# Second to fourth head group's queries and keys by a seven-product block scheme in one kernel for a hybrid attention and ConvFFN decoder layer

## What is computed

```
h = rms_norm(x, g_attn)                      # 256 x 2048
proj = h @ w_in                              # 2048 x (3*1024 + 8 + 3*1024 + 2*2048)
qa, ka, va, fa, qb, kb, vb, ga, gb = split(proj)
q_a, k_a = qk_norm(qa), qk_norm(ka)          # per head of 128, likewise q_b, k_b
o_a = fox_attention(q_a, k_a, va, log_sigmoid(fa + b_forget))      # 8 heads
o_b = dilated_attention(q_b, k_b, vb, slopes)                      # 8 heads
merged = sigmoid(ga) * (o_a @ w_br_fox) + sigmoid(gb) * (o_b @ w_br_dil)
x = x + merged @ w_out
x = x + conv_ffn(rms_norm(x, g_ffn))         # w_up 2048 x 11264, 3 taps, silu * val, w_down
```

## Time and profile before

| | |
|---|---|
| median of 3 runs | 1358.18 us (1357.86 to 1358.4) |
| time of the profiled execution | 1357.15 us |
| its span, first to last instruction | 1355.3 us |
| PE, PE weight loads, DVE, ACT, POOL busy | 1349.7, 1117.8, 1080.9, 831.5, 128.9 us |
| DMA | 299.45 MB, 221 GB/s mean |

### The profile page before, as it was taken

One profiled execution on the slowest core, in us unless ns is written; L12 is line 12 of the kernel. 1 busy time (PEld: TensorE's weight loads), 2 busy tenths in 40 slices (PEclk: granted clock), 3 DMA queues, 4 the chain that ended last, 5 costly groups with the idle time before them and its releaser, 6 DMA issues.

```text
span 1355.3 us, 16345 instructions
## 1 busy us (share of the span) xinstructions
PE 1349.7 (100%) x6144; PEld 1117.8 (82%) x6144; DVE 1080.9 (80%) x1320; ACT 831.5 (61%) x1038; POOL 128.9 (10%) x149
## 2 busy tenths in 40 slices
PE   9999999999999999999999999999999999999999
PEld 7888888888888888888888888888888888888887
DVE  6646555678878876657788999898999999999985
ACT  6655445466666654446776767666666666666762
POOL 0101010120111000001010101011110102010100
PEclk9999999999999999999999999999999999999999
DMA  9865555578888645567967988887979898888841
GB/s 344 247 203 170 168 174 170 155 219 233 205 229 230 221 168 175 200 228 226 297 149 292 235 293 222 261 245 210 278 197 286 198 291 181 308 187 282 222 179 62
DMA packets 115679, 299.45 MB, mean 221 GB/s; under 512 B 11656, under 2 KB 12944, under 8 KB 115088
## 3 DMA queue, kind: packets, MB, share of 16 engines
q1 hardware_dynamic: 95072, 241.92, 51.7%
q0 software_dynamic: 16448, 52.44, 22.1%
q10 hardware_dynamic: 4080, 4.05, 0.9%
HBM read 296.26 MB, written 2.11 MB: 220 GB/s over the span
## 4 chain that ended last, share of the span: by engine, by line
PE 99%; DMA 0%; ACT 0%; DVE 0%; issue 0%; SPq 0%; ACTq 0%
PE acc L643 17%; PE acc L645 17%; PE acc L644 16%; PE acc L676 7%; PE acc L680 7%; PE acc L678 7%; PE acc L661 3%; PE acc L665 3%; PE acc L663 3%; PE acc L881 2%; PE acc L883 2%; PE acc L885 2%; PE acc L856 2%; PE acc L858 2%; PE acc L860 2%; PE acc L969 1%
## 5 line engine op out<-in xcount | busy, mean ns | idle before, releaser
L1560 DVE TENSOR_TENSOR w_lo<-raw,w_hi 128x1024 fp32r<-128x1024 f32 x258 | 311.7, 1222 | 146.1 <-ACT w_hi L1133 144.8
L1133 ACT ACTIVATE w_hi<-raw 128x1024 fp32r<-128x1024 f32 x258 | 271.0, 1058 | 207.7 <-PE acc L645 173.8
L643 PE MATMUL acc<-w_hi,actA 128*128 128x512 f32 x856 | 339.7, 397 | 0.1
L645 PE MATMUL acc<-w_hi,actA 128*128 128x512 f32 x856 | 333.9, 390 | 0.0
L644 PE MATMUL acc<-w_lo,actA 128*128 128x512 f32 x856 | 333.2, 389 | 0.0
L645 PEld LDWEIGHTS acc<-w_hi,actA 128*128 128x128 f32 x856 | 160.7, 188 | 34.1
L643 PEld LDWEIGHTS acc<-w_hi,actA 128*128 128x128 f32 x856 | 160.8, 188 | 32.8 <-issue 1.0
L644 PEld LDWEIGHTS acc<-w_lo,actA 128*128 128x128 f32 x856 | 160.9, 188 | 32.2
L1133 ACT ACTIVATE w_hi<-raw_y 128x1024 fp32r<-128x1024 f32 x120 | 127.1, 1061 | 76.8 <-DMA raw_y<-w_in 18.2
L1560 DVE TENSOR_TENSOR w_lo<-raw_y,w_hi 128x1024 fp32r<-128x1024 f32 x120 | 145.2, 1220 | 24.3 <-ACT w_hi L1133 22.5
L1133 ACT ACTIVATE w_hi<-raw_x 128x1024 fp32r<-128x1024 f32 x90 | 95.2, 1059 | 55.6 <-PE acc L645 29.7
(11 more groups left out here) (259 smaller groups left out, 2264.9 us busy)
## 6 DMA issues: line engine op xcount, KB each, us to landing
raw<-w_in SPq DMA_DIRECT2D x126, 512.0 KB, 4.2
raw_x<-w_up SPq DMA_DIRECT2D x44, 512.0 KB, 5.7
raw<-w_down SPq DMA_DIRECT2D x42, 512.0 KB, 5.6
raw_y<-w_up POOLq DMA_DIRECT2D x35, 512.0 KB, 7.2
raw<-w_up SPq DMA_DIRECT2D x30, 512.0 KB, 7.0
raw<-w_out SPq DMA_DIRECT2D x28, 512.0 KB, 4.3
odd<-w_up SPq DMA_DIRECT2D x28, 512.0 KB, 4.4
work<-w_down SPq DMA_DIRECT2D x27, 512.0 KB, 5.1
```

What stands on the lines that cost most here:

```text
L643: nc.tensor.matmul(o, lhsT=a_h, rhs=w_hi[:, s, k, :], start=first and k == 0, stop=False)
L645: mm = nc.tensor.matmul(o, lhsT=a_l, rhs=w_hi[:, s, k, :], start=False, stop=last and k == KU - 1)
L1133: nc.scalar.activation(w_hi[:, n % RING, :, :], src.rearrange("p (k n) -> p k n", k=KU), ACT.Copy).then_inc(hi_done, 1)
L1560: nc.vector.tensor_tensor(w_lo[:, n % RING, :, :], src.rearrange("p (k n) -> p k n", k=KU), w_hi[:, n % RING, :, :].bitcast(f32), ALU.subt ...
```

## The change

The queries and keys of head groups 2 to 4 are no longer two plain rounds each. Each group's query and key columns (512 each) form a pair like those of the gates, so there are seven pairs (three of them before the gates' four), and in the first three the 22 units are followed by eight plain units V0 to V7 for the group's values. Only group 1 keeps its three rounds. The heads of group 1 are attended during the first pair, those of group 2 during the second, the dilated ones of group 3 during the third: scores behind units 2, 12, 19 and V2, the transposes of the probabilities behind units 5, 14, 21 and V4. Squares of the queries hang on unit 20 and of the keys on V3, their scaling on V0 and V4, the transposes behind V1, V2 and V5, V7. The block sums of the activations are made in the first group's rounds and two of them get a buffer of their own (`own_parts`). The decay rows move out of `raw_x` into `work`, and SP no longer waits for them. POOL's queue is reordered by hand. The reserve for POOL's DMA descriptors is set to 8192 bytes per partition. Cut to its core:

```diff
-FF0 = 31
...
-GATE_UNIT = 96
+GATE_UNIT = 24
+PAIRS = 7
...
-    for c in range(4):
+    for c in range(PAIRS):
...
+        if c < QK:
+            units += [("V", c, u) for u in range(UPR)]
...
+SCORES_AT = {("G", 0, 0): 0, ("H", "P5", 1): 1, ("H", "P4", 1): 2, ("V", 2): 3}
+TURN_AT = {("G", 0, 1): 0, ("G", 1, 0): 1, ("G", 1, 3): 2, ("V", 4): 3}
+VALUES_AT = {("H", "P6", 1): 0, ("G", 1, 1): 1, ("V", 1): 2, ("V", 6): 3}
+ROWS_AT = {("V", 1): (0, 0), ("V", 2): (0, 1), ("V", 5): (1, 0), ("V", 7): (1, 1)}
...
+ROUND_BANKS = ((2, 3), (0, 1), (2, 3))
...
+        own_parts = sb("own_parts", [P, 2 * HK * 2 * P], f32r)
...
+        decay_all = work[:, 4096:6144].rearrange("p (h s) -> p h s", s=SEQ)
+        decay = work[0:8, 3072:3072 + SEQ]
...
-            for g in range(GROUPS):
-                base = (0 if g < 2 else DIL_COL) + (g % 2) * NB
-                for m in range(3):
-                    if 3 * g + m > 1:
-                        round_of(3 * g + m, w_in_v, base + 1024 * m)
-            sp.wait_ge(prep_ready, prepared(7))
+            round_of(2, w_in_v, 2048)
...
-            pe.wait_ge(qn_done, 2 * GROUPS)
+            pe.wait_ge(qn_done, 2)
             for n, unit in enumerate(GATES, GATE_UNIT):
                 if unit[0] == "H":
                     gate_product(n, unit[1], unit[2], unit[3])
+                elif unit[0] == "G":
+                    gate_plain(n, unit[1], unit[2], unit[3])
                 else:
-                    gate_plain(n, unit[1], unit[2], unit[3])
+                    _, c, u = unit
+                    if u == 0:
+                        pe.wait_ge(g_c11, c + 1)
+                        pe.wait_ge(g_c21, c + 1)
+                    rows_unit(n, actA, (KU * u, KU * u + 1), (bank[gate_banks(c)[0]], bank[3]), u == 0, u == UPR - 1)
+                c, at = unit[1], place(unit)
+                if c >= QK:
+                    continue
+                if at in SCORES_AT:
+                    j = SCORES_AT[at]
+                    if j == 0:
+                        pe.wait_ge(qkt_done, 4 * (c + 1))
+                        pe.wait_ge(act_evac, c + 1)
+                    attend_scores(q_of(c)[:, j, :], lambda a, b: k_of(c)[:, j, a:b])
+                elif at in TURN_AT:
+                    attend_transpose(4 * c + TURN_AT[at])
+                if at in VALUES_AT:
+                    v, j = v_of(c), VALUES_AT[at]
+                    attend_values(4 * c + j, v[:, 0, j * P:(j + 1) * P], v[:, 1, j * P:(j + 1) * P])
+                if at in ROWS_AT:
+                    if ROWS_AT[at] == (0, 0):
+                        pe.wait_ge(g_c22, c + 1)
+                    transpose_heads(2 * (c + 1) + ROWS_AT[at][0], ROWS_AT[at][1])
 
...
+                elif unit == ("V", c, UPR - 1):
+                    act.wait_ge(used, n + 1)
+                    values_out(c + 1, (bank[gate_banks(c)[0]], bank[3]))
...
+            def squares(c, side):
+                act.wait_ge((g_c11, g_c12)[side], c + 1)
+                act.wait_ge((g_c21, g_c22)[side], c + 1)
+                act.wait_ge(qkt_ready, 2 * (2 * (c + 1) + side))
+                for r in range(RT):
+                    t = nc.scalar.activation(tmp[:, r, :], pair_sum(c, side, r), ACT.Square, scale=xrs[:, r:r + 1])
+                t.then_inc(sq_ready, 1)
 
             for n, unit in enumerate(GATES, GATE_UNIT):
                 gate_sum(n, unit)
                 high(n + RING)
-                _, c, kind, j = unit
+                c, at = unit[1], place(unit)
+                if c < QK:
+                    if at in SCORES_AT:
+                        exps(4 * c + SCORES_AT[at])
+                    elif at in TURN_AT:
+                        copy_pt(4 * c + TURN_AT[at])
+                    if at in VALUES_AT:
+                        out_high(4 * c + VALUES_AT[at])
+                    if at in ROWS_AT:
+                        turned_copy(c + 1, ROWS_AT[at][0], ROWS_AT[at][1])
+                    if at == ("G", 1, 2):
+                        squares(c, 0)
+                    elif at == ("V", 3):
+                        squares(c, 1)
+                    continue
                 if unit == ("G", c, 0, 1):
-                    if c:
-                        gate_sigmoid(c - 1, 0)
...
+                c, at = unit[1], place(unit)
+                if c < QK:
+                    if at in SCORES_AT:
+                        h = 4 * c + SCORES_AT[at]
+                        dve.wait_ge(prep_ready, prepared(h))
+                        softmax_head(h, prep, c == QK - 1)
+                    if at in VALUES_AT and 4 * c + VALUES_AT[at] < 10:
+                        out_low(4 * c + VALUES_AT[at])
+                    if at == ("G", 1, 2):
+                        head_sums(2 * (c + 1))
+                    elif at == ("V", 0):
+                        normalise(2 * (c + 1), [pair_sum(c, 0, r) for r in range(RT)])
+                    elif at == ("V", 3):
+                        head_sums(2 * (c + 1) + 1)
+                    elif at == ("V", 4):
+                        normalise(2 * (c + 1) + 1, [pair_sum(c, 1, r) for r in range(RT)])
+                elif unit == ("G", PAIRS - 1, 0, 2):
...
+            def third_sum(c, q):
+                pool.wait_ge(lo_done, GATE_AT["H", c, "P3", q])
+                add_pair_tile(c, q, raw_y[:, q, :], y_summed[q])
+
+            def first_sum(c, q):
+                pool.wait_ge(t2_added, QU * c + q + 1)
+                add_pair_tile(c, q, raw_x[:, q, :], x_summed[q])
+
+            third_sum(0, 0)
+            third_sum(0, 1)
+            for c in range(QK):
+                h = 4 * c
+                first_sum(c, 0)
+                first_sum(c, 1)
                 prepare(h + 1)
-                head_rms(2 * g)
                 prepare(h + 2)
                 prepare(h + 3)
-                head_rms(2 * g + 1)
+                head_rms(2 * (c + 1))
+                third_sum(c + 1, 0)
                 if h + 4 < 12:
                     prepare(h + 4)
-            prepare_dil(12).then_inc(prep_ready, 1)
-
-            def add_gate_tile(c, q, to, done):
-                col = GATE_COL + DM + NB * c
-                nc.gpsimd.dma_start(to.rearrange("p (k n) -> p k n", k=KU),
-                                    w_in_v[:, KU * q:KU * q + KU, col:col + NB], accum_op=ALU.add).then_inc(done, 16)
-
-            for n, unit in enumerate(GATES, GATE_UNIT):
-                _, c, kind, q = unit
-                if kind == "P3":
-                    pool.wait_ge(lo_done, n)
-                    add_gate_tile(c, q, raw_y[:, q, :], y_summed[q])
-                elif kind == "P7":
...
-    nc = bacc.Bacc("TRN2", target_bir_lowering=False, num_devices=1)
+    nc = bacc.Bacc("TRN2", target_bir_lowering=False, num_devices=1, dynamic_dma_scratch_size=8192)
```

More of the change, by code:

```diff
@@ L186, in sums_before @@
 def sums_before(i):
-    return QU * 4 + sum(quarters(b) for b in range(i))
+    return QU * PAIRS + sum(quarters(b) for b in range(i))
 X_PLAIN = WIDE_AT + MORE_SLOTS.index(6)
@@ L195 @@
 GATE_COL = DIL_COL + 3 * 1024
-assert FF_UNIT == OUT_UNIT + 3 * UPR
 S_ID = 0
@@ L337, in sum_at, with pair_sum @@
             return odd[:, m * HK * P:(m + 1) * HK * P].rearrange("p (k s) -> p k s", k=HK)
-        decay_all = raw_x[:, :, :].rearrange("p a (h s) -> p (a h) s", s=SEQ)
-        decay = raw_y[0:8, 0, 0:SEQ]
+        decay_all = work[:, 4096:6144].rearrange("p (h s) -> p h s", s=SEQ)
+        decay = work[0:8, 3072:3072 + SEQ]
+        def pair_sum(c, side, r):
+            if c >= QK:
+                return (ga, gb)[side][:, r, (c - QK) * NB:(c - QK + 1) * NB]
+            at = (3072, 6144)[side] + r * NB
+            return work[:, at:at + NB]
         a11, a21 = x2t[:, 0:HK, 0:P], x2t[:, 0:HK, P:SEQ]
@@ new lines, in _, with turned_copy @@
+            turned = {11: (0, 0), 12: (0, 1), 20: (1, 0), 22: (1, 1)}
+            def turned_copy(g, which, half):
+                nth = 2 * g + which
+                act.wait_ge(qkt_ready, 2 * nth + half + 1)
+                dst = (q_of(g), k_of(g))[which]
+                for jj in range(2):
+                    head = 2 * half + jj
+                    col = S_GQK + 4 * nth + head
+                    t = nc.scalar.activation(dst[:, head, :], bank[7][:, jj * SEQ:(jj + 1) * SEQ],
+                                             ACT.Copy, scale=smalls_sb[:, col:col + 1])
+                t.then_inc(qkt_done, 1)
@@ L1692, in _, with normalise @@
                     low(u)
-            def normalise(nth):
-                pair = 2 * ((3 * (nth // 2) + nth % 2) % 2)
+            def normalise(nth, rows):
                 dve.wait_ge(rs_ready, nth + 1)
@@ L1702, in normalise @@
                         tmp[:, r, :].rearrange("p (j d) -> p j d", j=4),
-                        bank[pair + r][:, :].rearrange("p (j d) -> p j d", j=4),
+                        rows[r].rearrange("p (j d) -> p j d", j=4),
```

(10 more changed lines are left out.)

454 lines of the change are left out of this document (215 added, 239 removed).

## The result

The changed kernel takes **1391.06 us** in the median of 4 runs (1390.17 to 1395.12), the kernel before 1358.29 (1357.86 to 1358.99, 4 runs). The ratio is 1.0247, with a 95% interval of 1.0226 to 1.0267: slower by 2.5%. I had said slower, but 1375 us, and 1383 with all upper ends. The sign and the places were right; the size was not. The profiled execution took 1395.12 us (span 1393.3), with a mean granted clock of 0.990; the other three had 0.992 to 0.994.

The account below looks back on a forecast made before the run. PE bounds the kernel, with 99% of the chain; waits (a) 11.8, (b) 7.3 and (c) 5.9, together 25.0, less 8.2 saved, give +16.8 us on 1357.15: 1374, or 1375 as median. Range 1362 to 1383.

Parts of the forecast that it names:

- all upper ends: Every wait at its upper bound (13.2 + 2.9 + 7.3 + 5.9 + 2) plus the clock's 2: 1383 us.
- The saved matmuls: Three query and key pairs at 180 instead of 192 matmuls: 36 fewer on PE, 8.2 us saved.
- (a): PE waits before each pair's first-head transposes, behind unit 5: 8.9, 0.8 and 2.1 us, together 11.8.
- The landing: First pair's third-sum adding DMA on POOL's queue, taken to land 6.0 us after its start; once 10.3 before.
- (b): PE waits before each pair's second-head transposes, behind unit 14: 2.0, 2.0 and 3.3 us, together 7.3.
- the reload of `raw_x`: Link in the second head's chain: ACT starts on the new tile 4.4 us after DVE is done.
- (c): PE waits before the key transposes behind V5: 1.75, 1.75 and 2.35 us, together 5.9; lower bound 4.0.
- the power: POOL's power in the keys' chain, taken as 1.65 us long from group 2's row.
- (d): Queries' chain (unit 20 to V1) called even, third dilated head at its limit: 0, upper bound 2 us.
- The clock: PE may fall to 1.2 GHz after standing still 9 us, making 1377 instead of 1375; left out of the sum.
- the reserve: Smaller POOL descriptor reserve, taken at zero; bounded by one more landing, 6 us.
- The 3 MB of added DMA: Two extra loads a pair where DMA share is 0.60: cost nothing, up to the landing times if they collide.

Follow-up runs that it names:

- experiment on POOL's order: Changed kernel with POOL issuing the first pair's two third-sum DMAs before the first head's bias instead of behind it: 1386.63 us, ratio 1.0207 to the kernel before.
- filled gaps: Changed kernel with 106 matmuls whose result nobody reads, placed before waiting transposes of four heads and the keys: 1387.06 us, ratio 1.0205 to the kernel before.
- all moves together: Changed kernel with POOL's third sum first, later head transposes, queries at V2 and V3, keys at V6: 1363.96 us, ratio 1.0042 to the kernel before.

## Why the prediction was right in sign and wrong in size

**The saved matmuls, 8.2 us.** Right, as far as the balance can tell: with it the table closes to a few us.

**(a) The first head, 11.8.** Right in place, order and releaser; measured 13.1. The landing took 7.7 us and not 6.0, with the DMA engines full; the other links agree within 0.6. The experiment on POOL's order shows the cause.

**(b) The second head, 7.3.** Measured 7.7 as a sum, but as 0.8, 2.4 and 4.5 and not 2.0, 2.0 and 3.3. In pair 1 the slow stretch behind the first gap let DVE catch up; the experiments on POOL's order and with filled gaps both bring it back to 2.1 to 2.4. The 4.5 of the dilated pair was undersized by 1.2 in this execution, in which the reload of `raw_x` took 5.1 us where I had 4.4; in the kernels where it took 3.4 and 3.8 the wait was 2.8 and 3.4, near my 3.3. That the sum is right is luck: the two errors of 1.2 cancel.

**(c) The keys, 5.9.** Mis-sized: 10.7. "ACT comes to V3 0.4 us late" was 1.25, and the power was taken at 1.65 us from one row where most of the trace's own rows say 2.5. Together that is 1.8 us in the first pair, where measured and forecast differ by 1.9; the other two differ by 1.5 each. The upper end of (c) was also its value, 5.9, so the range had nothing above it.

**(d) The queries and the third head, 0 with 2 as upper end.** Wrong: 3.1. Four gaps of 0.7 to 0.9. The prediction's own numbers leave the queries' chain 2.0 us of room (8.2 and 1.0 of PE's time against 7.2), and it calls that even; but the chain was mis-sized. In the first pair it took 9.8 us, from PE's end of unit 20 (136.1) to the end of the scaling (145.94):

```profile
137.34 1.05 ACT L1173 ACTIVATE w_hi<-raw 128x1024 fp32r<-128x1024 f32 x1
...
141.15 1.66 POOL L2158 TENSOR_TENSOR st<-st,smalls_sb 128x8 f32<-128x8 f32 x1 [3.70 <-DVE st L1810]
...
143.31 1.22 DVE L1619 TENSOR_TENSOR w_lo<-raw,w_hi 128x1024 fp32r<-128x1024 f32 x1
...
144.65 1.29 DVE L1759 TENSOR_TENSOR tmp<-work,st 128x512 f32<-128x512 f32 x2
```

ACT did the third head's exponentials first and came to its split at 137.34, some 1.0 us late. POOL's power ended at 142.81, but DVE has the split of a weight tile (143.31) ahead of the scaling in its order and began to scale at 144.65. The other two pairs and the third head were not followed link by link.

**The clock, left out of the sum.** This is the step that failed most: a term put at nothing that measured 8.4 us in the profiled execution. "While PE is slow DVE catches up for (b)" holds for the one stretch in pair 1 (1.1 us against 1.3 won back) and for none of the other four. I had thought of one gap of 9 us, and the low clock came behind waits from 2.2 us on. Six of my own forecast waits were 2 us and more, and at the 2.06 us of the earlier trace rows for each the sum would have been 1386 against this execution; I priced it once and then dropped it. (The 2.06 is itself a little high: 4.10 us over nine takes in the last matmul's own duration; the starts of the nine are 0.43 us apart behind the first, not 0.457.) That the clock falls because PE stands still is shown by the filled gaps. In the other three runs it was less: their mean clock was 0.992 to 0.994 instead of 0.990, which is at most 3 to 6 us of 1393, and they were 3.9 to 5.0 us shorter. How much of that is clock and how much an earlier landing can't be told, as they have no trace.

The misses are 8.4 for the clock, 4.8 for (c), 3.1 for (d), 1.3 for (a), 0.4 for (b) and 0.9 for L872, 18.9 of the 21.1 us between 1374 and 1395.12; the rest was not found. Against the medians (1375 and 1391.06) the miss is 16.1 us, and the list can't be drawn up, for want of a trace of a run near the median. The misses are all on one side: for the landing and for the power the trace had a short and a long row, and I took the short one. Of what I took at zero, the reserve is confirmed by its own run. The 3 MB of added DMA may have a part in the first pair's landing of 7.7 us and in the dilated pair's reload of 5.1; that was not told apart.

**What stays open.** Whether a schedule of these units exists that keeps some of the 8.2 us: two steps of closing the longest gap moved it on and gained nothing measurable. The wait at L872 in the second gate pair (0.5 to 1.5 us in most of the kernels, none in the one with filled gaps) was not followed to its cause. Why the wait of 3.1 us at 244.4 left the clock alone is not known.

## What to carry to other kernels

When work is packed more densely under a fixed order, count for each chain the time from its last input to PE's step, with the slower row where the trace has two for a link and with what else ACT and DVE have in their queues by then; a chain that is even is a gap. Where the sum forecasts waits of 2 to 3 us on PE, add the slow clock behind about half of them, and behind all that are clearly longer. And try the places before the arithmetic: one entry of a table, one unit later, was worth 13.3 us here, more than the whole change could save.

## What the runs showed of the hardware

- The low clock can begin behind a wait and not in it: PE restarted at 162.58 and its matmuls were at full pitch until 164.00. The length of the wait does not settle whether it comes: waits of 2.22 us (up to 204.09) and of 1.96 (in the kernel with filled gaps) had a slow stretch behind them, one of 3.13 (up to 244.44) and one of 2.17 (up to 95.06, in the experiment on POOL's order) had none. In all traces of this case together, of the waits that began at a full clock, none of the 25 of 1.0 to 1.8 us had a slow stretch in it or behind it, 12 of the 20 of 1.9 to 3.2 us had one, and all nine of 3.47 us and more.
- POOL's power on 8 columns takes 1.64 to 1.67 or 2.54 to 2.58 us and nothing between, in the traces before and after the change. It is the long one where a DVE split of 1.22 us had begun in the 0.2 us before it (158.24 and 158.41 above), the short one where that split began later or DVE had a sum of 0.69 us at that moment (141.15 above). The twelve traces of this case have 96 such powers, and all of them fit, with 2.66 as the longest; with all moves together the keys' power takes 1.67 in all three pairs, where the split begins 0.3 us or more behind it. It was not tested by itself.
